# Nine instead of seven pairs of the down projection by block products

## The chip, the cores and the metric

The kernel runs on one core of one Trainium2 chip. Times are device microseconds of one execution. The metric is the median of several executions.

## What is computed

Two transformer blocks over 256 positions of width 2048, all in float32: a first block with two attention layers, and a second one with a mixing layer and a feed-forward layer. The change touches the last product of the feed-forward layer, the down projection:

```python
h = rmsnorm(x, g_ffn[l])                                   # (256, 2048)
u = causal_dwconv(h @ w_up[l], ffn_conv_w[l]) + ffn_conv_b[l]
gate, val = jnp.split(u, 2, axis=-1)
x = x + (jax.nn.silu(gate) * val) @ w_down[l]              # (256, 5632) @ (5632, 2048)
return rmsnorm(x, g_final)
```

## The kernel before

Float32 precision is reached with two rounded parts of each operand. A tile of weights is loaded to a staging buffer, ScalarE rounds it (the part "hi"), VectorE subtracts that from the staged tile (the remainder, "lo"), and TensorE multiplies three passes: activations' hi with weights' hi, hi with lo, lo with hi. A pass is a matmul of a 128x128 block of activations with 128x512 of weights. The activations are in `act_T` with both parts.

The down projection has 44 tiles of 128 rows, taken as 22 row pairs, and 2048 columns, taken as two halves of 1024 (two quarters c of 512 each). PSUM holds 256 positions x 1024 columns at a time: banks `acc[0:2]` for the even quarter of the half, `acc[2:4]` for the odd one.

A pair is done in one of two ways in each half:

- in rows: two units, one for each quarter, each with two tiles x two position blocks x three passes = 12 matmuls. A half needs 24.
- by block products: the pair's 2x2 blocks of activations (two tiles x two position blocks) times its 2x2 blocks of weights (two tiles x two quarters) as seven products instead of eight, three passes each, 21 matmuls. Three products need sums of activation blocks (mixed blocks, `seven_T`, made by VectorE while the up projection of the pair runs, `ffn_sevens`), and four need sums of weight blocks (four VectorE adds of 128x512 in `rest_down`, the pair sums). The four units seven0 to seven3 have 6, 3, 6 and 6 matmuls. Four products go to banks of their own (`aux`), the other three to `acc`.

`DOWN_PAIRS` writes the order out by hand: a list is a group in rows (first all for the even quarter, then all for the odd one), a number is a pair by block products. `down_units` makes the flat list of units j from it. Each engine walks through that list:

- SyncE loads in order: each row unit to one of four staging buffers when the unit four before it has its remainder, each product pair (two transfers of 512 KB) to one of two pair buffers, when the product pair two before has its last remainder. The pair buffers lie where the up projection's activations were, and are free when that is over.
- ScalarE at step j rounds unit j+5 (at the beginning up to two units in a step, `prepared_at`), when its weights are there and TensorE is done with unit j+5-6. At the step after the last product of a half it copies a bank of products. At the step after a quarter's last unit it squares that quarter of x, behind VectorE's add.
- VectorE at step j makes the remainder of unit j+5 (`rest_down`, L692), and for seven1 the four pair sums (L697 to L701). At steps 0 to 2 it ends the last pair of the up projection. At the step after a half's last product it does four adds for the products (`add_sevens`, L2156 to L2159, behind ScalarE's copy), at the next one four more (L2161 to L2164). At a quarter's last unit it adds the two banks to x (`add_to_x`, L458), which frees them.
- TensorE waits for a unit's remainder, and before the first unit of each quarter of the second half also for the banks of the same quarter of the first half (`banks_free`). Before the first product of the second half it waits for `seven_free`, which the last of the eight adds gives.
- GpSimd loads the final gains into `gfin`, 1 MB over all partitions.

A `step(...)` around a VectorE instruction makes the next one wait until it has written.

Of the kernel before, what the change touches and what calls it, by code (L numbers as in the profile page):

```python
# [28 lines left out]
P = 128  # L29
# [93 lines left out]

OUT_PAIRS = [0, 1, 2, 6, 7, 3, 4, 5]

SEVEN = 7
DOWN_PAIRS = 2 * [[[7, 8, 9], 0, [10, 11], 1, [12, 13], 2, [14], 3, [15], 4, [16], 5, [17], 6, [18, 19, 20, 21]]]


def down_units():  # L130
# [70 lines left out]
def build(nc, dram, out):  # L201
# [12 lines left out]
    with ctx:  # L214
        def sb(name, shape, dt=F32, stack=ctx):
            return stack.enter_context(nc.sbuf_tensor("sb_" + name, shape, dt))

        def sem(name):
            return ctx.enter_context(nc.semaphore(name))
# [82 lines left out]
        gate_conv, gate_silu, act_ready = sem("gate_conv"), sem("gate_silu"), sem("act_ready")  # L302
        pair_staged = [sem("pair_staged0"), sem("pair_staged1")]
        sums_ready, first_copied, seven_free = sem("sums_ready"), sem("first_copied"), sem("seven_free")
        last_product = [sem("last_product0"), sem("last_product1")]
        last_added, final_rstd = sem("last_added"), sem("final_rstd")
        final_last = [sem("final_last0"), sem("final_last1")]
# [307 lines left out]
        mixing.close()  # L615


        ffn_tmp = sb("ffn_tmp", [P, 4, 2, SEQ])
        half3, sum3, gate, value = (ffn_tmp[:, i, :, :] for i in range(4))
        gfin = ffn_tmp[:, :, :, :].rearrange("p a c t -> p (a c t)")  # L620
        rb3 = turn_f32[:, 1, 0:T * P].rearrange("p (t k) -> p t k", t=T)
        rbc3 = turn_f32[:, 1, T * P:T * P + SEQ]
        act_T = sb("act_T", [P, FT, 2, SEQ], F32R)
# [79 lines left out]
        with nc.Block() as block:  # L703
# [95 lines left out]
            def _(pool):  # L799
# [77 lines left out]
                    pool.dma_start(pool_w[p0:p0 + n, i, :], w_rows[tile_ * P + p0:tile_ * P + p0 + n, :])\  # L877
                        .then_inc(mix_loaded, 16)

                pool.wait_ge(act_ready, N_FFN)  # L880
                pool.dma_start(gfin[:, :], dram["g_final_2"].partition_broadcast(P)).then_inc(gfin_loaded, 16)


# [1 line left out]
            def _(pe):  # L885
# [358 lines left out]
                def passes(o, a, j, part, start=False, stop=False):  # L1244


                    hi, lo = (ap[:, part * 512:(part + 1) * 512] for ap in down_slot(j))
                    pe.matmul(o, a(0), hi, start=start, stop=False)  # L1248
                    pe.matmul(o, a(0), lo, start=False, stop=False)  # L1249
                    return pe.matmul(o, a(1), hi, start=False, stop=stop)  # L1250
# [11 lines left out]
                def product_seven(j, first, last):  # L1262


                    _, i, _ = DOWN[j]
                    near = lambda k, t: lambda h: act_T[:, 2 * i + k, h, t * P:(t + 1) * P]
                    mixed = lambda n: lambda h: seven_T[:, i, h, n * P:(n + 1) * P]
                    pe.wait_ge(lo_ready, U4 + (j + 1))
                    passes(m_first, near(0, 0), j, 0, first, last)
                    passes(acc[:, 2, :], mixed(2), j, 1).then_inc(unit_used, 1)  # L1270
                    pe.wait_ge(lo_ready, U4 + (j + 2))
                    passes(acc[:, 0, :], near(1, 0), j + 1, 0).then_inc(unit_used, 1)
                    pe.wait_ge(lo_ready, U4 + (j + 3))
                    passes(m_fifth, mixed(0), j + 2, 0, first, last)
                    passes(m_seventh, near(0, 1), j + 2, 1, first, last).then_inc(unit_used, 1)
                    pe.wait_ge(lo_ready, U4 + (j + 4))
                    passes(m_sixth, mixed(1), j + 3, 0, first, last)
                    passes(acc[:, 1, :], near(1, 1), j + 3, 1).then_inc(unit_used, 1)

                for j, (kind, i, c) in enumerate(DOWN[:DOWN_TAIL]):  # L1280
                    if c == 0:
                        pe.wait_ge(act_ready, i + 1)
                    if kind == "rows":
                        first = j == min(r for r in DOWN_ROWS if DOWN[r][2] == c)
                        if first:
                            banks_free(pe, PAIRS4, c)
                        product_down(j, first, j == DOWN_END[c])
                    if kind == "seven0":
                        if j == SEVEN_FIRST[SEVEN]:
                            pe.wait_ge(seven_free, 1)  # L1290
                        product_seven(j, j in (SEVEN_FIRST[0], SEVEN_FIRST[SEVEN]), j + 3 == SEVEN_END[c])
                for t in range(T):
                    o = acc[:, 2 + t, :]
                    for j in range(DOWN_TAIL, U_DOWN):
# [326 lines left out]
            def _(dve):  # L1621
# [527 lines left out]
                def add_sevens(chunk, late):  # L2149
# [10 lines left out]
                    else:  # L2160
# [3 lines left out]
                        dve.tensor_tensor(x_high[1], m_fifth, x_high[1], ALU.add).then_inc(seven_free, 1)  # L2164
                        dve.wait_ge(seven_free, chunk + 1)

                for j in range(U_DOWN):
                    for ahead in prepared_at(j):
                        rest_down(step, dve, ahead)
                    if j == 0:  # L2170
                        ffn_sums(N_FFN, 1, 1)
                    if j == 1:
                        ffn_conv(N_FFN, 1, 1)
                    if j == 2:
                        ffn_act(N_FFN, 1)
                    if j - 1 in SEVEN_END:
                        add_sevens(SEVEN_END.index(j - 1), False)
                    if j - 2 in SEVEN_END:
                        add_sevens(SEVEN_END.index(j - 2), True)
                    if j in DOWN_END[:3]:  # L2180
                        c = DOWN_END.index(j)
                        add_to_x(dve, U4, j, c % 2, c)
# [56 lines left out]
```

## Time and profile before

| | |
|---|---|
| median of 3 runs | 1946.02 us (1945.85 to 1946.25) |
| the profiled execution | 1946.43 us, its span 1944.6 us |
| TensorE busy | 1928.8 us (99%) |
| VectorE busy | 1371.4 us (71%) |
| ScalarE busy | 1047.4 us (54%) |
| down projection | 1704.6 to 1934.6 us of the span |

The span goes from the first to the last instruction. TensorE's matmuls overlap in the records (0.39 us each, a new one every 0.23 us), so their pace is read from start to start.

### The profile page before, as it was taken

The page shows a single profiled execution, that of the slowest core. Times are in us where ns is not written, and L with a number is a line of the kernel's source. Part 1 is how long each engine was busy: PE and PEld are TensorE (multiplying, and loading weights), DVE is VectorE, ACT ScalarE, POOL GpSimd, SP SyncE. Part 2 cuts the span into 40 slices and gives each one's busy share as a digit, 9 for nine tenths or more (in the row PEclk, how much of TensorE's full clock was granted, in tenths as well). Part 3 has the DMA queues.
Part 4 walks back from the last instruction along what each step waited for, and adds up shares of the span by engine and source line. Part 5 has one row for each costly group of instructions (what it writes and reads, how often), then busy time and mean ns, then how long its engine had stood idle before and what let it go on. Part 6 is the DMA issues. An engine that isn't in the chain of part 4 may idle for free.

```text
span 1944.6 us, 27002 instructions
## 1 busy us (share of the span) xinstructions
PE 1928.8 (99%) x9818; PEld 1635.5 (84%) x9818; DVE 1371.4 (71%) x1941; ACT 1047.4 (54%) x1533; POOL 46.4 (2%) x73
## 2 busy tenths in 40 slices
PE   8999999999999999999999999999999999999997
PEld 7888888888888888888888888888888888888886
DVE  7755675656655675656768766888877887888787
ACT  5533676654433676664544544555555555555554
POOL 1000030000000020000100000000000000000000
PEclk9999999999999999999999999999999999999999
DMA  8666545556666555545666545565656566676653
GB/s 310 205 194 194 151 145 160 151 157 186 187 194 192 146 162 174 153 151 180 213 193 188 158 164 186 182 193 184 194 185 193 185 189 188 191 240 203 219 188 117
DMA packets 246964, 357.06 MB, mean 184 GB/s; under 512 B 15318, under 2 KB 136496, under 8 KB 246364
## 3 DMA queue, kind: packets, MB, share of 16 engines
q1 hardware_dynamic: 245148, 349.08, 58.3%
q0 software_dynamic: 1584, 6.54, 1.0%
q8 instruction: 55, 0.90, 0.2%
q14 instruction: 33, 0.27, 0.0%
q10 hardware_dynamic: 144, 0.26, 0.0%
HBM read 352.69 MB, written 3.16 MB: 183 GB/s over the span
## 4 chain that ended last, share of the span: by engine, by line
PE 98%; DMA 1%; DVE 1%; ACT 0%; issue 0%; SPq 0%; ACTq 0%
PE acc L410 22%; PE acc L387 16%; PE acc L389 15%; PE acc L388 15%; PE acc L403 11%; PE acc L1249 3%; PE acc L1250 3%; PE acc L1248 3%; PE aux L467 2%; PE aux L964 1%; DMA sb_stage<-w_kv 1%; PE aux L1249 1%; PE aux L1250 1%; PE aux L1248 1%; PE aux L982 1%; PE aux L945 1%
## 5 line engine op out<-in xcount | busy, mean ns | idle before, releaser
L350 DVE TENSOR_TENSOR sb_w_lo<-sb_stage,sb_w_hi 128x1024 fp32r<-128x1024 f32 x567 | 694.3, 1227 | 377.0 <-ACT sb_w_hi L345 369.9
L345 ACT ACTIVATE sb_w_hi<-sb_stage 128x1024 fp32r<-128x1024 f32 x567 | 598.5, 1058 | 501.5 <-PE acc L389 248.9
L410 PE MATMUL acc<-sb_xT,sb_w_hi 128*128 128x512 f32 x1856 | 445.7, 391 | 0.0
L410 PEld LDWEIGHTS acc<-sb_xT,sb_w_hi 128*128 128x128 f32 x1856 | 340.8, 188 | 65.8
L387 PE MATMUL acc<-sb_w_hi,sb_xT 128*128 128x512 f32 x768 | 305.7, 398 | 0.0
L389 PE MATMUL acc<-sb_w_hi,sb_xT 128*128 128x512 f32 x768 | 299.5, 390 | 0.0
L388 PE MATMUL acc<-sb_w_lo,sb_xT 128*128 128x512 f32 x768 | 299.3, 390 | 0.0
L403 PEld LDWEIGHTS acc<-sb_xT,sb_w_lo 128*128 128x128 f32 x1856 | 238.7, 191 | 9.3
L403 PE MATMUL acc<-sb_xT,sb_w_lo 128*128 128x256 f32 x1856 | 243.0, 283 | 0.0
L387 PE MATMUL acc<-sb_w_hi,sb_mT 128*128 128x512 f32 x560 | 224.7, 401 | 0.8 <-DVE sb_mT L490 0.7
L389 PE MATMUL acc<-sb_w_hi,sb_mT 128*128 128x512 f32 x560 | 218.6, 390 | 0.0
L388 PE MATMUL acc<-sb_w_lo,sb_mT 128*128 128x512 f32 x560 | 218.4, 390 | 0.0
L389 PEld LDWEIGHTS acc<-sb_w_hi,sb_xT 128*128 128x128 f32 x768 | 144.2, 188 | 30.8
L387 PEld LDWEIGHTS acc<-sb_w_hi,sb_xT 128*128 128x128 f32 x768 | 144.3, 188 | 28.7
L388 PEld LDWEIGHTS acc<-sb_w_lo,sb_xT 128*128 128x128 f32 x768 | 144.4, 188 | 27.7
L387 PEld LDWEIGHTS acc<-sb_w_hi,sb_mT 128*128 128x128 f32 x560 | 105.2, 188 | 24.3 <-DVE sb_mT L490 1.3
L389 PEld LDWEIGHTS acc<-sb_w_hi,sb_mT 128*128 128x128 f32 x560 | 105.1, 188 | 22.9
L388 PEld LDWEIGHTS acc<-sb_w_lo,sb_mT 128*128 128x128 f32 x560 | 105.3, 188 | 20.0
L2064 DVE SCALAR_TENSOR_TENSOR sb_ffn_tmp<-sb_ffn_tmp,sb_taps 128x254 f32<-128x254 f32 (+1 forms) x176 | 77.3, 481 | 2.5
L1248 PE MATMUL acc<-sb_w_hi,sb_act_T 128*128 128x512 f32 x192 | 74.7, 389 | 0.0
L1249 PE MATMUL acc<-sb_w_lo,sb_act_T 128*128 128x512 f32 x192 | 74.7, 389 | 0.0
L1250 PE MATMUL acc<-sb_w_hi,sb_act_T 128*128 128x512 f32 x192 | 74.7, 389 | 0.0
(335 smaller groups left out, 1910.5 us busy)
## 6 DMA issues: line engine op xcount, KB each, us to landing
sb_stage<-w_in SPq DMA_DIRECT2D x248, 512.0 KB, 3.9
sb_stage<-w_up SPq DMA_DIRECT2D x176, 512.0 KB, 3.7
sb_stage<-w_out SPq DMA_DIRECT2D x96, 512.0 KB, 4.2
sb_stage<-w_down SPq DMA_DIRECT2D x60, 512.0 KB, 7.0
sb_pair_stage<-w_down SPq DMA_DIRECT2D x28, 512.0 KB, 6.9
sb_stage<-w_kv SPq DMA_DIRECT2D x16, 512.0 KB, 6.8
sb_stage<-w_ukv SPq DMA_DIRECT2D x16, 512.0 KB, 4.0
sb_stage<-w_uq SPq DMA_DIRECT2D x12, 512.0 KB, 3.6
```

The source lines that it names most:

```text
L345: act.activation(w_hi[:, j % RING, 0:size], stage[:, j % RING, 0:size], ACT.Copy).then_inc(hi_ready, 1)
L350: dve.tensor_tensor(w_lo[:, j % RING, 0:size], stage[:, j % RING, 0:size], w_hi[:, j % RING, 0:size].bitcast(F32), ALU.subtract).then_inc( ...
L387: pe.matmul(o, x_hi, hi[:, k, :], start=first and k == 0, stop=False)
L388: pe.matmul(o, x_hi, lo[:, k, :], start=False, stop=False)
L389: mm = pe.matmul(o, x_lo, hi[:, k, :], start=False, stop=last and k == nk - 1)
L403: mm = pe.matmul(acc[:, 2 * pair + c, 0:SEQ], lo[:, k, c * P:(c + 1) * P], xT[:, k0 + k, 0, :], start=False, stop=False)
L410: mm = pe.matmul(acc[:, 2 * pair + c, :], hi[:, k, c * P:(c + 1) * P], both, start=first and k == 0, stop=last and k == 3)
L467: mm = pe.transpose(aux[:, bank, i * P:(i + 1) * P], src(i), ident[:, :])
L1248: pe.matmul(o, a(0), hi, start=start, stop=False)
L1249: pe.matmul(o, a(0), lo, start=False, stop=False)
L1250: return pe.matmul(o, a(1), hi, start=False, stop=stop)
L2064: last = dve.scalar_tensor_tensor(out=y[:, k, d:SEQ], in0=sum3[:, k, 0:SEQ - d], scalar=taps[:, 2 - d, half, k:k + 1], in1=y[:, k, d:SEQ], ...
```

## The change

Nine instead of seven pairs are done by block products in each half. The order is another one: single pairs in rows stand between all products, and the last group of the first half has two pairs instead of four. The mixed blocks of pairs 7 and 8 are not made in the up projection but at steps 4 and 5 of the down stage, by `mix_late`, from the finished activations (hi + lo). They go to a buffer `late_T`, which lies where `ffn_tmp` was. The final gains, which were loaded there, go to the first pair buffer, when the last product pair but one has its last remainder.

```diff
@@ -123,8 +123,9 @@
 
 OUT_PAIRS = [0, 1, 2, 6, 7, 3, 4, 5]
 
-SEVEN = 7
-DOWN_PAIRS = 2 * [[[7, 8, 9], 0, [10, 11], 1, [12, 13], 2, [14], 3, [15], 4, [16], 5, [17], 6, [18, 19, 20, 21]]]
+SEVEN, LATE = 7, 2
+DOWN_PAIRS = [[[9, 10, 11], 0, [12], 1, [13], 2, [14], 3, [15], 4, [16], 5, [17], 6, [18], 7, [19], 8, [20, 21]],
+              [[9], 0, [10], 1, [11], 2, [12], 3, [13], 4, [14], 5, [15], 6, [16], 7, [17], 8, [18, 19, 20, 21]]]
 
 
 def down_units():
@@ -302,6 +303,7 @@
         gate_conv, gate_silu, act_ready = sem("gate_conv"), sem("gate_silu"), sem("act_ready")
         pair_staged = [sem("pair_staged0"), sem("pair_staged1")]
         sums_ready, first_copied, seven_free = sem("sums_ready"), sem("first_copied"), sem("seven_free")
+        late_mixed = sem("late_mixed")
         last_product = [sem("last_product0"), sem("last_product1")]
         last_added, final_rstd = sem("last_added"), sem("final_rstd")
         final_last = [sem("final_last0"), sem("final_last1")]
@@ -615,9 +617,12 @@
         mixing.close()
 
 
+        late = ExitStack()
+        late_T = sb("late_T", [P, LATE, 2, 4 * P], F32R, late)
+        late.close()
         ffn_tmp = sb("ffn_tmp", [P, 4, 2, SEQ])
         half3, sum3, gate, value = (ffn_tmp[:, i, :, :] for i in range(4))
-        gfin = ffn_tmp[:, :, :, :].rearrange("p a c t -> p (a c t)")
+        gfin = pair_stage[:, 0, :, :].rearrange("p a n -> p (a n)")
         rb3 = turn_f32[:, 1, 0:T * P].rearrange("p (t k) -> p t k", t=T)
         rbc3 = turn_f32[:, 1, T * P:T * P + SEQ]
         act_T = sb("act_T", [P, FT, 2, SEQ], F32R)
@@ -877,7 +882,7 @@
                     pool.dma_start(pool_w[p0:p0 + n, i, :], w_rows[tile_ * P + p0:tile_ * P + p0 + n, :])\
                         .then_inc(mix_loaded, 16)
 
-                pool.wait_ge(act_ready, N_FFN)
+                pool.wait_ge(lo_ready, U4 + (SEVEN_FIRST[-2] + 4))
                 pool.dma_start(gfin[:, :], dram["g_final_2"].partition_broadcast(P)).then_inc(gfin_loaded, 16)
 
 
@@ -1264,7 +1269,13 @@
 
                     _, i, _ = DOWN[j]
                     near = lambda k, t: lambda h: act_T[:, 2 * i + k, h, t * P:(t + 1) * P]
-                    mixed = lambda n: lambda h: seven_T[:, i, h, n * P:(n + 1) * P]
+                    if i < SEVEN:
+                        mixed = lambda n: lambda h: seven_T[:, i, h, n * P:(n + 1) * P]
+                        a_third = near(0, 1)
+                    else:
+                        pe.wait_ge(late_mixed, i - SEVEN + 1)
+                        mixed = lambda n: lambda h: late_T[:, i - SEVEN, h, n * P:(n + 1) * P]
+                        a_third = mixed(3)
                     pe.wait_ge(lo_ready, U4 + (j + 1))
                     passes(m_first, near(0, 0), j, 0, first, last)
                     passes(acc[:, 2, :], mixed(2), j, 1).then_inc(unit_used, 1)
@@ -1272,7 +1283,7 @@
                     passes(acc[:, 0, :], near(1, 0), j + 1, 0).then_inc(unit_used, 1)
                     pe.wait_ge(lo_ready, U4 + (j + 3))
                     passes(m_fifth, mixed(0), j + 2, 0, first, last)
-                    passes(m_seventh, near(0, 1), j + 2, 1, first, last).then_inc(unit_used, 1)
+                    passes(m_seventh, a_third, j + 2, 1, first, last).then_inc(unit_used, 1)
                     pe.wait_ge(lo_ready, U4 + (j + 4))
                     passes(m_sixth, mixed(1), j + 3, 0, first, last)
                     passes(acc[:, 1, :], near(1, 1), j + 3, 1).then_inc(unit_used, 1)
@@ -1286,9 +1297,9 @@
                             banks_free(pe, PAIRS4, c)
                         product_down(j, first, j == DOWN_END[c])
                     if kind == "seven0":
-                        if j == SEVEN_FIRST[SEVEN]:
+                        if j == SEVEN_FIRST[SEVEN + LATE]:
                             pe.wait_ge(seven_free, 1)
-                        product_seven(j, j in (SEVEN_FIRST[0], SEVEN_FIRST[SEVEN]), j + 3 == SEVEN_END[c])
+                        product_seven(j, j in (SEVEN_FIRST[0], SEVEN_FIRST[SEVEN + LATE]), j + 3 == SEVEN_END[c])
                 for t in range(T):
                     o = acc[:, 2 + t, :]
                     for j in range(DOWN_TAIL, U_DOWN):
@@ -2164,9 +2175,29 @@
                         dve.tensor_tensor(x_high[1], m_fifth, x_high[1], ALU.add).then_inc(seven_free, 1)
                         dve.wait_ge(seven_free, chunk + 1)
 
+                def mix_late(n):
+
+
+                    i = SEVEN + n
+                    whole, four = turn_f32[:, 0, :], turn_f32[:, 1, :]
+                    step(dve.tensor_tensor(whole.rearrange("p (k t) -> p k t", k=2),
+                                           act_T[:, 2 * i:2 * i + 2, 0, :].bitcast(F32),
+                                           act_T[:, 2 * i:2 * i + 2, 1, :].bitcast(F32), ALU.add))
+                    a11, a21, a12, a22 = (whole[:, k * P:(k + 1) * P] for k in range(4))
+                    first, second, fourth, third = (four[:, k * P:(k + 1) * P] for k in range(4))
+                    step(dve.tensor_tensor(first, a21, a22, ALU.subtract))
+                    dve.tensor_tensor(third, a11, a21, ALU.subtract)
+                    step(dve.tensor_tensor(second, a11, first, ALU.subtract))
+                    step(dve.tensor_tensor(fourth, a12, second, ALU.subtract))
+                    step(dve.tensor_scalar(late_T[:, n, 0, :], four, 1.0, None, ALU.mult))
+                    dve.tensor_tensor(late_T[:, n, 1, :], four, late_T[:, n, 0, :].bitcast(F32), ALU.subtract)\
+                       .then_inc(late_mixed, 1)
+
                 for j in range(U_DOWN):
                     for ahead in prepared_at(j):
                         rest_down(step, dve, ahead)
+                    if j in (4, 5):
+                        mix_late(j - 4)
                     if j == 0:
                         ffn_sums(N_FFN, 1, 1)
                     if j == 1:
```

## Rows read from the trace of the kernel before

**Rows 1.** The page: busy times, the chain that ended last; TensorE's waits.

```profile
PE 1928.8 (99%) x9818; PEld 1635.5 (84%) x9818; DVE 1371.4 (71%) x1941; ACT 1047.4 (54%) x1533; POOL 46.4 (2%) x73
...
PE 98%; DMA 1%; DVE 1%; ACT 0%; issue 0%; SPq 0%; ACTq 0%
...
PE acc L387 <- DVE sb_mT L490: 0.7, 1, 0.7
```

**Rows 2.** Timeline of TensorE, down stage: start, length, instruction, tiles, shapes, count.

```profile
1704.61 0.39 PE L1248 MATMUL acc<-sb_w_hi,sb_act_T 128*128 128x512 f32 x1
...
1725.69 0.39 PE L1248 MATMUL acc<-sb_down_hi,sb_act_T 128*128 128x512 f32 x1
...
1797.77 0.39 PE L1248 MATMUL acc<-sb_w_hi,sb_act_T 128*128 128x512 f32 x1
...
1934.23 0.39 PE L1303 MATMUL acc<-sb_w_hi,sb_act_T 128*128 128x512 f32 x1
```

**Rows 3.** Windows: length, busy PE, PEld, DVE, ACT, POOL (count), clock, DMA, GB/s.

```profile
1715.00:1725.00 10.00, 10.00 (x45) 8.26 (x45) 9.86 (x11) 6.44 (x7) 0.56 (x1) 1.00 0.69 256
...
1765.00:1775.00 10.00, 10.00 (x46) 8.29 (x45) 9.12 (x10) 5.51 (x7) 0.00 (x0) 1.00 0.67 207
```

**Rows 4.** Timeline of VectorE, regular pattern: remainders and pair sums of a product pair.

```profile
1765.13 1.83 DVE L692 TENSOR_TENSOR sb_down_lo<-sb_pair_stage,sb_down_hi 128x1024 fp32r<-128x1024 f32 x2
1766.99 0.69 DVE L697 TENSOR_TENSOR sb_pair_stage<-sb_pair_stage 128x512 f32<-128x512 f32 x1
...
1769.17 0.69 DVE L701 TENSOR_TENSOR sb_pair_stage<-sb_pair_stage 128x512 f32<-128x512 f32 x1
1769.78 2.44 DVE L692 TENSOR_TENSOR sb_w_lo<-sb_pair_stage,sb_w_hi 128x1024 fp32r<-128x1024 f32 x2
```

**Rows 5.** Timeline of VectorE: mixing in the up projection; last activations of the stage.

```profile
1312.89 0.29 DVE L2081 TENSOR_TENSOR sb_turn_f<-sb_ffn_tmp 128x128 f32<-128x128 f32 x1
1313.22 0.29 DVE L2082 TENSOR_TENSOR sb_turn_f<-sb_ffn_tmp,sb_turn_f 128x128 f32<-128x128 f32 x1
...
1713.58 0.43 DVE L2097 TENSOR_SCALAR sb_act_T<-sb_ffn_tmp 128x512 fp32r<-128x512 f32 x1
1714.05 0.69 DVE L2098 TENSOR_TENSOR sb_act_T<-sb_ffn_tmp,sb_act_T 128x512 fp32r<-128x512 f32 x1
1714.65 1.82 DVE L692 TENSOR_TENSOR sb_w_lo<-sb_pair_stage,sb_w_hi 128x1024 fp32r<-128x1024 f32 x2
```

**Rows 6.** Timeline of VectorE, start of the stage: remainders 10 and 11.

```profile
1721.65 2.36 DVE L692 TENSOR_TENSOR sb_down_lo<-sb_stage,sb_down_hi 128x1024 fp32r<-128x1024 f32 x2
```

**Rows 7.** Timelines of VectorE and TensorE: the one wait of TensorE for VectorE.

```profile
9.55 0.69 DVE L490 TENSOR_TENSOR sb_mT<-sb_turn_f,sb_mT 128x512 fp32r<-128x512 f32 x1
...
10.29 0.50 PE L387 MATMUL acc<-sb_w_hi,sb_mT 128*128 128x512 f32 x1 [0.74 <-DVE sb_mT L490]
10.63 0.39 PE L388 MATMUL acc<-sb_w_lo,sb_mT 128*128 128x512 f32 x1
```

**Rows 8.** Timelines, change of halves: ScalarE's rounding (again at the second half's end), VectorE.

```profile
1800.80 1.06 ACT L685 ACTIVATE sb_w_hi<-sb_stage 128x1024 fp32r<-128x1024 f32 x1 [2.38 <-DMA sb_stage<-w_down]
...
1803.04 0.68 DVE L2156 TENSOR_TENSOR sb_turn_f<-aux,sb_turn_f 128x512 f32<-128x512 f32 x1
...
1809.97 1.22 DVE L692 TENSOR_TENSOR sb_w_lo<-sb_stage,sb_w_hi 128x1024 fp32r<-128x1024 f32 x1
...
1812.25 1.28 DVE L458 TENSOR_TENSOR sb_x<-acc,sb_x 128x512 f32<-128x512 f32 x2
1813.44 1.22 DVE L692 TENSOR_TENSOR sb_down_lo<-sb_stage,sb_down_hi 128x1024 fp32r<-128x1024 f32 x1
...
1915.75 1.06 ACT L685 ACTIVATE sb_down_hi<-sb_stage 128x1024 fp32r<-128x1024 f32 x1 [2.35 <-DMA sb_stage<-w_down]
```

**Rows 9.** DMA issues in the down stage: the final gains.

```profile
sb_ffn_tmp<-g_final POOLq DMA_DIRECT2D x1, 1024.0 KB, 7.5
```

**Rows 10.** Window at the end, columns as in rows 3.

```profile
1936.75:1937.00 0.25, 0.00 (x0) 0.00 (x0) 0.22 (x2) 0.00 (x0) 0.00 (x0) 0.50 1.06 426
```

## The prediction

> **What bounds the kernel now.** I read the chain that ended last first: TensorE carries 98% of it, and the summary line of busy times has it busy for 1928.8 of 1944.6 us [rows 1]. A busy TensorE is not yet a TensorE at its pace, so I looked for its waits: in the whole program one is listed against another engine, 0.7 us at the very beginning. The single matmuls of the down projection confirm it [rows 2]. Its first one starts at 1704.61 and the 94th at 1725.69, so one takes 21.08 / 93 = 0.2267 us. The stage has 2 x (7 x 21 + 15 x 24) = 1014 of them (seven block products of three passes for a pair that is done so, 24 matmuls for any other, in each half of the columns); 1014 x 0.2267 = 229.9 us lead from 1704.61 to 1934.5, and the last one does start at 1934.23. There is no gap in this stage, so a matmul taken out is worth its 0.2267 us, as long as what feeds TensorE keeps up. The feeder is VectorE: in ten us of the regular pattern (one pair by products, one in rows) it is busy 9.12 us, and in ten us of the start 9.86 [rows 3]. Where the order gives it less time, it comes last.
>
> I count units as the code does (j from 0 in the down stage). In rows a unit is 12 matmuls, 2.72 us; the four units of a product pair are 6, 3, 6 and 6 matmuls: 1.36, 0.68, 1.36 and 1.36 us, 4.76 together.
>
> **Part 1, fewer matmuls.** Two more pairs of 22 are done with 21 instead of 24, in both halves: 2 x 2 x 3 = 12 matmuls less, 12 x 0.2267 = **-2.72 us**.
>
> **Part 2, the start of the stage.** Units 0 to 9 (six in rows, then pair 0) are the same in both orders. Then the old one has four units in rows, the new one two, and VectorE gets the two mixings between its units 9 and 10 and between 10 and 11. Length of a mixing: an add of 128x512 whose successor waits for it (0.727, the pitch of the pair sums: three of them in 2.18 us) [rows 4], three subtractions of 128x128 with such a wait (0.325 each) and one without (the pitch of an instruction that nobody waits for is its length less 0.09, as 0.69 gives 0.60: 0.29 gives 0.20), a rounding of 0.47 and a rest of 0.60 [rows 5]. Sum 2.97 us, twice 5.94 us. Before, the two unit remainders 10 and 11 follow at once at 1721.65, 1.14 us apart [rows 6]. The new ledger follows. TensorE starts 0.05 us after its operand is there, and the first matmul after a wait takes 0.34 instead of 0.23 us (0.69 us from 9.55 ends at 10.24, starts are 10.29 and 10.63) [rows 7], so every wait costs 0.11 beside its length.
> - Mixing to 1724.62, remainder 10 ready 1725.84; TensorE wants it at 1725.69: +0.20 + 0.11 = 0.31.
> - Mixing to 1728.73, remainder 11 ready 1729.96; wanted at 1725.69 + 0.31 + 2.72 = 1728.72: +1.29 + 0.11 = 1.40.
> - Remainder 12 from 1729.87, remainder 13 and the four pair sums (from its start to the next remainder 1769.78 - 1765.13 - 1.14 = 3.5) [rows 4], remainder 14 ready 1735.75. Wanted at 1732.84 + 1.36 + 0.68 = 1734.88: +0.92 + 0.11 = 1.03.
> - Remainder 15 ready at 1737.0, wanted 1737.27; from here VectorE gains about 1 us in every pattern of 10.2 us.
>
> Together **+2.74 us**. Bounds: 0, if VectorE had the mixings in idle time (it has next to none there [rows 3]), and 3.7 if each of the ten waits inside the mixings costs 0.1 more.
>
> The page "VectorE: DVE Perf Modes" of the Trainium skill, section "The DRAIN you can't avoid", says that a semaphore after every instruction costs nothing against one after the last. The trace disagrees: 0.73 from start to start with the wait, 0.60 without [rows 4, 5]. By the page a mixing would be 2.36 us, the start 1.5 instead of 2.74, and the whole 1.2 us less than I forecast.
>
> **Part 3, the change of halves.** This is the largest term. T is the end of the last product of the first half: 1797.77 in the trace [rows 2]. Four PSUM banks hold the sums of two column quarters, and a quarter of the second half can't begin before VectorE has added the same banks' old sums to x. The old order has 8 units in rows after T, so these banks are wanted at T + 21.8 and T + 29.9. The new one has 4, then the first unit of each new quarter: wanted at T + 10.88 and T + 13.60. VectorE's work from T on is known [rows 8]: the four adds of the products start at T + 5.27 (ScalarE's copy comes behind the rounding of the sixth unit after T, whose weights land at T + 3.0), a remainder behind them at T + 8.2, four more adds end at T + 12.20. In the new order the add of the first quarter follows there, 1.28 long: banks free T + 13.48, TensorE resumes 13.53. Wait 2.65 + 0.11 = **2.76**. The unit that runs then ends at 10.88 + 2.76 + 2.72 = T + 16.36. The other quarter's add waits in VectorE's order behind the 0.69 remainder and the four pair sums of the new half's first pair (from T + 13.39, 3.50) and another remainder (1.14): start T + 18.03, free T + 19.31. Wait 19.36 - 16.36 + 0.11 = **3.11**. Sum **+5.87 us**. What is queued behind, the next products, finds its operands ready (T + 9.4, 14.1, 18.1, 20.4 for units wanted from T + 22.2). Bounds: if those weights landed early, VectorE would begin 2.7 us sooner and the sum be 3.2; if the second add is late by another remainder, 7.1. I take 5.87, since the order of loads up to that point is the same and its nearest row shows the same landing.
>
> **What costs nothing.** The final gains move from a buffer that the mixings now use to a staging buffer; the 1 MB takes 7.5 us [rows 9] and now starts about 30 us before VectorE reads it, with POOL idle. SyncE's pair loads wait for the same event as before; the tightest by the ledger is pair 3's, issued at 1737.0 when remainder 15 frees its buffer and wanted at 1745.7, behind the product of pair 2's first unit: with 7 us to landing it is 1.7 us early, and up to 1 us may come of the row units queued behind it. The new wait for the mixed blocks comes some 65 us after the mixings. End of the stage: the same eight units, the same tail of 10.1 us.
>
> **Sum.** -2.72 + 2.74 + 5.87 = +5.9 us. The profiled execution took 1946.43 us (span 1944.6) and the median of the runs is 1946.02, 0.4 below; from the median 1951.9 us.
>
> **Rivals.**
> - The clock: TensorE stands still for 2.7 and 3.1 us with one unit between them. At the end of the trace the granted clock falls to the lower of its two levels (0.50 of 2.4 GHz) some 2 us after TensorE's last matmul has ended at 1934.6, or sooner [rows 10]. So it may fall here. The unit between the waits is covered by the second; after it one unit at half pace costs 2.7 us more, a half of it as the middle: 1953.3, at most 1954.6. Against: no row shows when it comes back, nor a fall inside the program.
> - The weights of the sixth unit after T land as soon as they are wanted (the wait for a transfer is gone with another traffic): Part 3 is 3.2, total +3.2, 1949.2. Against: the landing at the second half's end, 1915.75, is again 3.1 us behind the last product (411 matmuls after the 507 of the first half end at 1912.7) [rows 8].
> - The other sign: VectorE keeps up everywhere, and only the matmuls count: 1943.3. For it: VectorE is busy 71% of the program, and its lead in the regular pattern is 3.7 us (a remainder ready at 1771.0 [rows 4] for a unit wanted 309 matmuls into the stage, at 1774.7). It decides from the point where the bank adds come before T + 10.9 and the mixings fit in the lead at unit 10, which is 2.8 us before the change. Both fail in the ledgers.
> - The start is as forecast but the change of halves costs nothing, for instance because the adds to x are placed earlier than I read: 1946.0, no change.
>
> "Perfetto Trace Analysis" of the Trainium skill, section "Identifying the Most-Contended Engine", takes occupancy as the measure of a vector engine's room. By that rule the third of these holds, 1943.3 us. The trace's 9.12 of 10 us and the order of single instructions speak against it.
>
> **Chances.** Forecast 0.45, clock 0.25, early weights 0.12, only matmuls 0.08, start alone 0.10. A measurement of this kernel tells about 0.2% (3.9 us) from no change, so slower begins at 1949.9 and faster ends at 1942.1. Slower: forecast, clock and a third of the early weights, 0.74. Faster: half of the matmuls' case, 0.04, should a little more come with them. Same: the rest, 0.22. The range goes from 1949.0 (early weights) to 1954.8 (one unit at half pace).
>
> **What would show it.** TensorE's waits inside the down stage: three short ones at 1725 to 1736 on VectorE's remainders (sum 2.7), two at 1813 to 1830 on VectorE's adds to x (2.7 and 3.0). 1002 matmuls of the stage. The last matmul starting near 1940.1. The granted clock at 1.00 there. Wrong if the waits at the change of halves are missing or over 4 us, or if there is a wait in the regular pattern, which would be a transfer or VectorE's pace.

## The result, and the profile after

The changed kernel takes 1951.0 us (median of 11, 1949.9 to 1952.7), the one before 1946.1 us (median of 11, 1945.5 to 1947.9). The ratio is 1.0028, 95% interval 1.002 to 1.0036: slower by 4.9 us, forecast 5.8, and inside the range. The profiled execution's span is 1949.0 us, 4.4 above the span before.

TensorE's waits for VectorE in the profile after, for the whole program (waiting line, releaser, us in all, times, longest), stand against one of 0.7 us before, at its very beginning [rows 1]. Both programs also wait once for the first load (4.4 and 4.9 us), and the changed one 0.2 us for a transfer ahead of the down projection.

```profile
PE acc L1253 <- DVE sb_x L460: 4.0, 2, 2.6
PE acc L1253 <- DVE sb_down_lo L697: 1.0, 1, 1.0
PE aux L1253 <- DVE sb_w_lo L697: 0.7, 1, 0.7
```

Two on an add to x (L460 is L458 of before), two on a remainder (L697, before L692). The start of the stage on VectorE, answering to [rows 5, 6]; the first mixing goes from 1720.96 to 1723.93:

```profile
1720.96 0.68 DVE L2183 TENSOR_TENSOR sb_turn_f<-sb_act_T 128x512 f32<-128x512 f32 x1
1721.68 0.29 DVE L2188 TENSOR_TENSOR sb_turn_f<-sb_turn_f 128x128 f32<-128x128 f32 x1
1722.01 0.29 DVE L2189 TENSOR_TENSOR sb_turn_f<-sb_turn_f 128x128 f32<-128x128 f32 x1
1722.22 0.28 DVE L2190 TENSOR_TENSOR sb_turn_f<-sb_turn_f 128x128 f32<-128x128 f32 x1
...
1723.32 0.69 DVE L2193 TENSOR_TENSOR sb_late_T<-sb_turn_f,sb_late_T 128x512 fp32r<-128x512 f32 x1
1723.93 1.22 DVE L697 TENSOR_TENSOR sb_down_lo<-sb_stage,sb_down_hi 128x1024 fp32r<-128x1024 f32 x1
```

That is 2.97 us, as forecast, with the pitch of 0.2 where no wait stands (1722.01 to 1722.22) and 0.33 with one. TensorE's timeline beside it, the last matmul before each wait and the first behind it, answering to [rows 2]:

```profile
1724.79 0.39 PE L1255 MATMUL acc<-sb_w_hi,sb_act_T 128*128 128x512 f32 x1
1725.30 0.47 PE L1253 MATMUL acc<-sb_down_hi,sb_act_T 128*128 128x512 f32 x1
...
1727.91 0.39 PE L1255 MATMUL acc<-sb_down_hi,sb_act_T 128*128 128x512 f32 x1
1729.31 0.50 PE L1253 MATMUL acc<-sb_down_hi,sb_act_T 128*128 128x512 f32 x1 [1.01 <-DVE sb_down_lo L697]
...
1734.02 0.39 PE L1255 MATMUL acc<-sb_w_hi,sb_act_T 128*128 128x512 f32 x1
1735.09 0.50 PE L1253 MATMUL aux<-sb_w_hi,sb_seven_T 128*128 128x512 f32 x1 [0.68 <-DVE sb_w_lo L697]
```

The gap is start to start less the pace of 0.23: 0.28, 1.17 and 0.84, with 0.07, 0.11 and 0.11 behind them. A few matmuls behind these are some hundredths late as well, as the sum over the stretch below shows.

Then the change of halves. T, the end of the last product of the first half, is 1809.34 here, where the first matmul in rows starts. ScalarE's rounding of the sixth unit behind it waits for its weights to T + 3.15 (1812.49), and VectorE's adds follow, answering to [rows 8]:

```profile
1812.49 1.06 ACT L690 ACTIVATE sb_w_hi<-sb_stage 128x1024 fp32r<-128x1024 f32 x1 [2.46 <-DMA sb_stage<-w_down]
...
1813.58 1.23 DVE L697 TENSOR_TENSOR sb_w_lo<-sb_stage,sb_w_hi 128x1024 fp32r<-128x1024 f32 x1 [2.30 <-ACT sb_w_hi L690]
1814.72 0.69 DVE L2167 TENSOR_TENSOR sb_turn_f<-aux,sb_turn_f 128x512 f32<-128x512 f32 x1
...
1821.66 1.29 DVE L460 TENSOR_TENSOR sb_x<-acc,sb_x 128x512 f32<-128x512 f32 x2
...
1827.50 1.28 DVE L460 TENSOR_TENSOR sb_x<-acc,sb_x 128x512 f32<-128x512 f32 x2
```

and TensorE:

```profile
1809.34 0.39 PE L1253 MATMUL acc<-sb_down_hi,sb_act_T 128*128 128x512 f32 x1
...
1819.99 0.39 PE L1255 MATMUL acc<-sb_w_hi,sb_act_T 128*128 128x512 f32 x1
1823.00 0.79 PE L1253 MATMUL acc<-sb_w_hi,sb_act_T 128*128 128x512 f32 x1 [2.62 <-DVE sb_x L460]
1823.59 0.63 PE L1254 MATMUL acc<-sb_w_lo,sb_act_T 128*128 128x512 f32 x1
...
1827.06 0.40 PE L1255 MATMUL acc<-sb_w_hi,sb_act_T 128*128 128x512 f32 x1
1828.84 0.50 PE L1253 MATMUL acc<-sb_w_hi,sb_act_T 128*128 128x512 f32 x1 [1.39 <-DVE sb_x L460]
```

The first unit after the first wait is long: its matmuls are 0.43 us apart, and the granted clock says why (windows, columns as in rows 3):

```profile
1822.00:1822.50 0.50, 0.00 (x0) 0.00 (x0) 0.50 (x2) 0.00 (x0) 0.00 (x0) 1.00 0.00 0
1822.50:1823.00 0.50, 0.00 (x0) 0.00 (x1) 0.50 (x2) 0.02 (x1) 0.00 (x0) 0.67 0.00 0
1823.00:1824.00 1.00, 1.00 (x2) 0.83 (x3) 0.97 (x2) 0.97 (x3) 0.00 (x0) 0.50 0.00 0
...
1826.00:1827.00 1.00, 1.00 (x5) 0.79 (x5) 1.00 (x2) 0.65 (x2) 0.00 (x0) 0.96 0.00 0
```

The stage as a whole, with two matmuls behind the waits (the 151st, and the 25th behind the one at 1819.99):

```profile
1703.93 0.39 PE L1253 MATMUL acc<-sb_w_hi,sb_act_T 128*128 128x512 f32 x1
...
1740.66 0.39 PE L1253 MATMUL acc<-sb_down_hi,sb_act_T 128*128 128x512 f32 x1
...
1831.71 0.39 PE L1253 MATMUL aux<-sb_down_hi,sb_act_T 128*128 128x512 f32 x1
...
1939.60 0.39 PE L1314 MATMUL acc<-sb_w_hi,sb_act_T 128*128 128x512 f32 x1
```

At the pace of 0.2267 us, 150 matmuls take 34.00 us and here took 36.73: the start costs 2.73. And 25 take 5.67 and took 11.72: the change of halves costs 6.05. From the first start to the last the stage is 235.67 us against 229.62: +6.05 again, where the steps of the prediction sum to 5.9. The span shows less for two reasons. This execution came 0.7 us sooner to the stage (0.5 of it since its first load landed at 4.4 instead of 4.9 us). And its tail, from the last matmul's start to the end, is 9.4 instead of 10.4 us. This shorter tail is in the profile of every kernel that has the new code for the mixings (9.4 to 9.5 us, in one 10.0), and in neither of the two without it (10.4): a term that the prediction missed, looked at below under the tail. 6.05 - 0.95 = 5.1 us is then what the median should show, and it shows 4.9. The eleven times lie in two groups, six from 1949.9 to 1951.0 and five from 1952.2 to 1952.7, and the median is the highest of the lower group: one more time in the upper one, and it would have been 1952.2. What divides them is looked at under the scatter and the clock.

### The profile page after: what moved, and what is told of

Read it like the earlier page. It is cut to its first block, busy times and chain, and to the rows that moved or that the text cites. A ratio compares the mean times of both kernels' runs of the same rounds, so it can differ in the third digit from the quotient of the medians.

```text
span 1949.0 us, 27032 instructions
## 1 busy us (share of the span) xinstructions
PE 1929.6 (99%) x9806; PEld 1635.3 (84%) x9806; DVE 1394.7 (72%) x1979; ACT 1051.8 (54%) x1541; POOL 46.3 (2%) x73
## 4 chain that ended last, share of the span: by engine, by line
PE 96%; DVE 3%; DMA 0%; ACT 0%; issue 0%; SPq 0%; ACTq 0%
PE acc L412 22%; PE acc L389 16%; PE acc L391 16%; PE acc L390 16%; PE acc L405 11%; PE aux L469 2%; PE acc L1253 2%; PE acc L1254 2%; PE acc L1255 2%; PE aux L1253 1%; PE aux L1254 1%; PE aux L1255 1%; PE aux L969 1%; PE aux L950 1%; PE aux L987 1%; PE aux L986 1%
## 5 line engine op out<-in xcount | busy, mean ns | idle before, releaser
L690 ACT ACTIVATE sb_w_hi<-sb_pair_stage 128x1024 fp32r<-128x1024 f32 (+1 forms) x54 | 52.4, 986 | 67.5 <-DVE sb_pair_stage L703 57.3
L697 DVE TENSOR_TENSOR sb_w_lo<-sb_pair_stage,sb_w_hi 128x1024 fp32r<-128x1024 f32 (+1 forms) x54 | 60.3, 1132 | 0.4
L1571 ACT ACTIVATE sb_ffn_tmp<-sb_ffn_tmp,sb_taps 128x256 f32<-128x256 f32 x88 | 48.1, 595 | 17.9 <-DVE sb_ffn_tmp L2067 17.1
```

The costliest lines, as they stand in the source:

```text
L697: dve.tensor_tensor(lo, src, hi.bitcast(F32), ALU.subtract).then_inc(lo_ready, 1)
```

## The experiments

In the tables and below, "stage" is the time from the start of the down projection's first matmul to that of its last, read in TensorE's timeline of each profile. It leaves out the scatter ahead of the stage and behind it. The kernels were timed in turn with the kernel before, 6 to 11 times each; the two single runs only once.

| kernel | stage, us | stage against before | median, us | before beside it |
|---|---|---|---|---|
| before | 229.62 |  | 1946.1 |  |
| changed | 235.67 | +6.05 | 1951.0 | 1946.1 |
| changed again | 235.60 | +5.98 | 1951.1 | 1946.1 |
| changed, two single runs | 236.72, 236.73 | +7.10, +7.11 | 1952.3, 1951.7 | 1946.1 |
| mixings at 30 and 42 | 236.24 | +6.62 | 1951.7 | 1946.1 |
| short group alone | 234.99 | +5.37 | 1952.8 | 1946.1 |
| mixings alone | 231.40 | +1.78 | 1947.1 | 1946.1 |
| mixings at 12 and 30 | 232.64 | +3.02 | 1949.3 | 1946.0 |
| adds first | 231.53 | +1.91 | 1947.0 | 1946.0 |
| both | 228.77 | -0.85 | 1944.3 | 1946.0 |
| room | 227.90 | -1.72 | 1943.8 | 1946.0 |
| copy first | 234.73 | +5.11 | 1950.4 | 1946.1 |
| room, copy first | 226.89 | -2.73 | 1942.6 | 1946.1 |

**The start alone.** The old order and number of products, with the two mixings at steps 4 and 5:

```diff
-DOWN_PAIRS = [[[9, 10, 11], 0, [12], 1, ...
+DOWN_PAIRS = 2 * [[[7, 8, 9], 0, [10, 11], 1, [12, 13], 2, [14], 3, ..., 6, [18, 19, 20, 21]]]
```

> The kernel before in order and number of products, with the two mixings of the change at steps 4 and 5, their results not used, and the final gains in the pair buffer. Theory: the first two waits of the start ledger, 0.31 and 1.40 us; the third is gone, since units 12 and 13 are in rows: 1.7 us more than before, 1947.8 us. Rival 1: the four units in rows give VectorE room and the mixings cost nothing, 1946.1. Rival 2: moving the final gains costs at the end of the stage, then a wait near 1929 us, and more than 2 us.

Stage +1.78 us, with two waits of 0.28 and 1.29 us and their 0.08 each: the ledger's first two, and not its third. The median is 1.1 us above before (ratio 1.0005, 0.9996 to 1.0014), which its interval does not tell from nothing, so it is the stage that carries this verdict; 1.8 less 0.95 of the tail would be 0.8. Moving the final gains left no wait at the end: rival 2 is out.

**The change of halves alone.** The kernel before with its rows in another order:

```diff
-DOWN_PAIRS = 2 * [[[7, 8, 9], 0, [10, 11], 1, [12, 13], 2, [14], 3, [15], 4, [16], 5, [17], 6, [18, 19, 20, 21]]]
+DOWN_PAIRS = [[[7, 8, 9], 0, [10, 11], 1, [12, 13], 2, [14, 15], 3, [16, 17], 4, [18], 5, [19], 6, [20, 21]],
+              [[7], 0, [8, 9], 1, [10, 11], 2, [12, 13], 3, [14, 15], 4, [16], 5, [17], 6, [18, 19, 20, 21]]]
```

> The kernel before (seven pairs by products, no mixing in the stage) with the order of its rows changed alone: two instead of four pairs stand behind the last product of the first half, one instead of three at the beginning of the second. The same matmuls, the same VectorE work. Theory (the banks are wanted before VectorE has added them to x): two waits of TensorE for the adds to x, 2.76 and 3.11 us, 5.9 us more than before, about 1952.0 us (1953.6 where the clock stays low). Rival (VectorE's load of two more product pairs in each half is what costs): the load is that of before, the time 1946.1.

1952.8 us, ratio 1.0033 (1.0021 to 1.0045), with the same 1014 matmuls and the same VectorE work. The stage is 5.4 us longer, and TensorE's timeline has just two waits, both for the adds to x (L459 here):

```profile
1821.18 0.59 PE L1249 MATMUL acc<-sb_down_hi,sb_act_T 128*128 128x512 f32 x1 [1.93 <-DVE sb_x L459]
...
1827.02 0.50 PE L1249 MATMUL acc<-sb_down_hi,sb_act_T 128*128 128x512 f32 x1 [1.24 <-DVE sb_x L459]
```

So the place of the four units in rows costs this, not the two further products. The profile is of the shortest of the six executions (1951.39), and its stage with the tail of before accounts for it; the median is 1.4 us above it, and no trace shows one of the longer ones.

**Mixings later.** In the changed kernel:

```diff
-                    if j in (4, 5):
+                    if j in (30, 42):
```

> The changed kernel with the two mixings at steps 30 and 42 instead of 4 and 5. Theory: VectorE has about 3.7 us of lead there, a mixing takes 2.95, so the three waits at the start go and nothing new comes: 2.7 us less than the changed kernel, about 1948.3 us, five waits become two. Rival (the order itself, with single pairs in rows from the start, is too dense for VectorE): the start waits stay and the time is that of the changed kernel, 1951; second rival: the lead is used up at the new place, a wait of 1 to 2 us appears there, and the gain is 1 us.

A miss. The three waits at the start did go, and a wait of 0.25 us came at pair 7. But the time stayed, 1951.7: the wait for the first bank had grown.

```profile
1818.18 0.39 PE L1255 MATMUL acc<-sb_w_hi,sb_act_T 128*128 128x512 f32 x1
1824.00 0.80 PE L1253 MATMUL acc<-sb_w_hi,sb_act_T 128*128 128x512 f32 x1 [5.43 <-DVE sb_x L460]
```

ScalarE's timeline of the same profile shows the way there; T is 1807.5, and the last three roundings before the copy (L1613) all wait for weights:

```profile
1807.65 1.06 ACT L690 ACTIVATE sb_w_hi<-sb_stage 128x1024 fp32r<-128x1024 f32 x1 [0.22 <-DMA sb_stage<-w_down]
1810.46 1.06 ACT L690 ACTIVATE sb_w_hi<-sb_stage 128x1024 fp32r<-128x1024 f32 x1 [1.74 <-DMA sb_stage<-w_down]
1813.49 1.06 ACT L690 ACTIVATE sb_w_hi<-sb_stage 128x1024 fp32r<-128x1024 f32 x1 [1.97 <-DMA sb_stage<-w_down]
1814.45 0.58 ACT L1613 ACTIVATE sb_turn_f<-aux 128x512 f32<-128x512 f32 x1
```

The mixing at step 42 had put VectorE's remainders back. These free the staging buffers: the one that frees the sixth unit's buffer ended at T - 0.1 instead of T - 2.2, the load went out 2.1 us later, and it landed at T + 6.0 instead of T + 3.1. I took the second mixing away from there:

```diff
-                    if j in (4, 5):
+                    if j in (12, 30):
```

> The changed kernel with the mixings at steps 12 and 30. With the second one at step 42 the three waits at the start went, but the wait for the first bank grew from 2.8 to 5.6 us. Theory A: the mixing at 42 took VectorE's lead two patterns ahead of the change of halves, a pair load stood behind it in SyncE's order with the row loads behind that, and the sixth unit's weights landed at T + 6.0 instead of T + 3.0. With the second mixing at 30 the lead is there again: waits at the start 0 (some tenths at most), at the change of halves 2.8 and 3.1 (the second shorter by the slow unit), the stage 232.9 us, 2.7 less than in the changed kernel, time 1948.4 (1950 where the clock stays low). Rival B: at the change of halves VectorE has a fixed amount of work to do by a fixed time, and the waits at the start only moved it; then the first bank's wait grows again by what the start saves, and the time is 1951.

Stage 232.64, 3.0 us less than the changed kernel; the only waits left are the two for the banks, 2.5 and 1.4 us with a slow unit between. Median 1949.3. The sixth unit's weights landed at T + 2.8. Theory A holds, rival B falls: the start's waits are worth their length, if the second mixing stands where the lead can be won back. With four product pairs still to come in the half (step 30) it was, with two (step 42) it was not; no place between was tried.

**The order at the change of halves.** In VectorE's program (the same calls leave their old places further down, not shown; ScalarE's squares of the two quarters go behind, with a wait for `seven_free`):

```diff
+                    if j == SEVEN_END[0] + 2:
+                        add_to_x(dve, U4, DOWN_END[0], 0, 0)
+                    if j == SEVEN_END[0] + 3:
+                        add_to_x(dve, U4, DOWN_END[1], 1, 1)
+                        dve.wait_ge(acc_free[1], PAIRS4 + 1)
+                        add_sevens(0, True)
                     for ahead in prepared_at(j):
                         rest_down(step, dve, ahead)
```

> The changed kernel with VectorE's order at the change of halves turned: the adds of the first quarter to x directly behind the first four adds of the products, those of the second quarter before the last four, ScalarE's squares of both later. VectorE's work is the same. Theory: bank 0 is free at T + 9.4 (wanted 10.9) and bank 1 at T + 12.4 (wanted 13.6), so both waits go; the last four adds end at T + 15.2, the pair sums follow, and the new half's first product waits for its third unit: wanted T + 18.4, ready 19.9, 1.7 us with its 0.11. The start waits stay. In all 4.2 us less than the changed kernel, about 1946.9 us, no clock fall. Rival: the banks are not it but the work VectorE has to do between the halves; then 5.9 us of waits stay in another place, 1951.

1947.0 us, stage 231.53 (expected 231.5). Both waits for the banks are gone, and in their place stands the one that was expected, for the third unit of the first product:

```profile
1829.82 0.50 PE L1253 MATMUL aux<-sb_w_hi,sb_seven_T 128*128 128x512 f32 x1 [1.57 <-DVE sb_w_lo L697]
```

The banks were it. Both edits together:

> Both edits, mixings at 12 and 30 and the adds to x first. Theory: the terms add up: -2.72 for the matmuls and the 1.7 left at the change of halves, 1.0 us less than before: about 1945.1 us. Rival: what one edit saves the other loses; 1947 or more.

1944.3 us, stage 228.77, 0.85 less than before; 0.95 of the tail comes to it, and the median is 1.7 less (ratio 0.9992, 0.9983 to 1.0001, which alone does not tell it from no change). Then the room in front of the second half's first product (pair 6's load goes out one row unit earlier, and the last four adds of the products stand between the two adds to x again):

```diff
-              [[9], 0, [10], 1, [11], 2, [12], 3, [13], 4, [14], 5, [15], 6, [16], 7, ...
+              [[9, 10], 0, [11], 1, [12], 2, [13], 3, [14], 4, [15], 5, 6, [16], 7, ...
```

> As both edits, and in the second half pairs 9 and 10 in rows stand before the first product, while the products of pairs 5 and 6 follow each other without rows between (pair 6's load is then issued one row unit earlier). The last four adds of the products come before the second quarter's add again. Theory: bank 0 free T + 9.4 (wanted 10.9), bank 1 free T + 15.7 (wanted 16.3), the product's third unit ready T + 21.4 (wanted 23.8): no wait at the change of halves, and the double product takes 2.1 us of VectorE's lead of 3.7. Only the 12 matmuls are left: 2.7 us less than before, 1943.4 us. Rival: the double product or its loads make a wait of 1 to 3 us, 1945 to 1946.

1943.8 us, ratio 0.9989 (0.998 to 0.9998). The double product makes no wait. But the ledger missed 1.0 us of the stage: TensorE still waits 0.56 + 0.11 for the second bank, since VectorE starts its adds at T + 6.3 here and not at T + 5.3, and 0.16 + 0.11 at 1925, at the end of the second half. VectorE is late there too: its last add of bank sums to x starts 1.6 us behind the last matmul's start, and 1.0 in the kernel with the copy first as well, and by this 0.55 us the tail of this kernel is longer.

**The late weights.** ScalarE's copy and VectorE's first four adds go ahead of the sixth unit:

```diff
+                    if j - 1 in SEVEN_END:
+                        multiplied(act, U4, j - 1)
+                        act.activation(first_f, m_first, ACT.Copy).then_inc(first_copied, 1)
                     for ahead in prepared_at(j):
                         round_down(act, ahead)
```

> The changed kernel, with ScalarE's copy of a product bank at the end of a half put ahead of the rounding that waits for the weights landing at T + 3.0, and VectorE's first four adds ahead of that unit's remainder. Theory (the 2.8 us for late weights are a term of both waits at the change of halves): the adds start at T + 0.9 instead of T + 5.3, bank 0 is free at T + 10.5 (wanted 10.9, no wait), bank 1 at T + 16.4 (wanted 13.6): one wait of 2.9 us instead of 2.8 and 3.1. Start waits as before. 3.0 us less than the changed kernel: about 1948.3 us, stage 232.7 us. Rival (VectorE's amount of work sets it, its start does not): no change, 1951.2.

A hit in the waits and a miss in the time. The waits are 0.51 + 0.11 and 2.98 us: the weights are a term of the first one, as forecast, but 0.6 is left, for VectorE stood one unit earlier than I had it (the fifth unit's remainder comes first and waits for its own weights; the adds start at T + 2.0, not 0.9). The stage is 234.73, not 232.7, since there is this 0.6, and since the matmuls behind the second wait run at the lower clock in this profile (1.3 us). The 11 times lie in two groups, 1948.5 to 1948.6 (three) and 1950.2 to 1951.4 (eight): the lower one is where the expectation was, but no trace shows one of the three. With the room it leaves nothing:

> The kernel with both edits and room before the first product (1943.8 us, one wait of 0.7 us left for the second bank), and the copy first as well. Theory: bank 1 is free 3 us sooner, that wait goes, the stage is 1002 matmuls without a gap, 227.1 us, and the time 1943.1 us. Rival: the copy first delays the sixth unit's rounding and a wait comes there; 1943.8 or more.

1942.6 us (1942.2 to 1942.8), ratio 0.9982 (0.9973 to 0.9991), 3.5 us faster than before. Of TensorE's waits in the whole program only the one for the first load is left, and 1001 x 0.2267 is 226.9:

```profile
PE acc L894 <- DMA sb_qb<-par_rows: 4.8, 1, 4.8
```

**The tail.** In the profiled executions the span ends 10.4 us behind the start of the last matmul in the kernel before and in the one with the short group alone, and 9.4 to 9.5 us in all others but "room" (10.0). The difference between 10.4 and 9.4 arises behind ScalarE's last instruction, which ends 5.7 us behind the last matmul's start in either; so the final gains' new place is not its cause. The DMA view of the last 8 us (queues with packets, MB, share; then issues with the us to landing), first of the kernel with the short group alone, whose program is that of before in all else:

```profile
q14 instruction: 1, 0.01, 0.8%
...
out<-sb_x SPq DMA_DIRECT2D x3, 256.0 KB, 2.7
out<-sb_x ACTq DMA_DIRECT2D x1, 256.0 KB, 3.2
```

then of the changed one, where the queue of instruction loads has no packet in this stretch:

```profile
out<-sb_x SPq DMA_DIRECT2D x3, 256.0 KB, 2.3
out<-sb_x ACTq DMA_DIRECT2D x1, 256.0 KB, 2.8
```

With a load of instructions among the last stores (its packet starts 6.7 us behind the last matmul's start and takes 1.0 us), the first store lands as before, the next two 0.4 us later, the last one 1.0 us later, and so does the end; the kernel before has the same packet and the same 3.2. In the kernel with the mixings alone the packet comes 1.5 us ahead of the last matmul's start, and the tail is 9.4. That the packet is the cause, and that the longer program moved it away, is argued from this coincidence over the profiles; no kernel was made to test it alone.

**The scatter and the clock.**

> The changed kernel once more, for the spread of its times (they lie in two groups, near 1950.8 and near 1952.4 us). Theory (VectorE is late at two places): five waits of TensorE in the down stage as predicted, 2.7 us in all at the start and 5.9 us at the change of halves, in every execution. The clock falls during the first wait for the banks and comes back before the second one ends, which costs nothing in the profiled execution; in the executions of the upper group it comes back late or falls again in the second wait, and some 8 matmuls behind it start 0.43 instead of 0.23 us apart, +1.6 us. Rival: the spread comes from the landings of the weights; then the waits themselves differ between the groups.

> The changed kernel, one look for the spread of its times (1950 to 1952.7 us, while kernels without the waits for banks spread half as wide). If the time is over 1952: theory, the waits are the same and matmuls behind the second wait run at the lower clock; rival, a wait is longer. If it is under 1951.5: the clock is back before the second wait ends.

> A second look at the changed kernel, with the same expectations: over 1952 us with matmuls at the lower clock behind the second wait (theory) or with a longer wait (rival); under 1951.5 us with neither.

The first profile was taken at 1951.15 us and shows what the first one of the change showed. The single runs, at 1952.25 and 1951.68, show the other kind. From TensorE's timeline (T is 1809.63), ScalarE's rounding of the sixth unit and the windows of the first of them:

```profile
1809.63 0.39 PE L1253 MATMUL acc<-sb_down_hi,sb_act_T 128*128 128x512 f32 x1
...
1822.72 0.50 PE L1253 MATMUL acc<-sb_w_hi,sb_act_T 128*128 128x512 f32 x1 [2.04 <-DVE sb_x L460]
...
1828.55 0.69 PE L1253 MATMUL acc<-sb_w_hi,sb_act_T 128*128 128x512 f32 x1 [2.78 <-DVE sb_x L460]
1829.04 0.63 PE L1254 MATMUL acc<-sb_w_lo,sb_act_T 128*128 128x512 f32 x1
...
1831.60 0.63 PE L1254 MATMUL acc<-sb_w_lo,sb_act_T 128*128 128x512 f32 x1
```

```profile
1812.20 1.06 ACT L690 ACTIVATE sb_w_hi<-sb_stage 128x1024 fp32r<-128x1024 f32 x1 [1.90 <-DMA sb_stage<-w_down]
```

```profile
1823.00:1824.00 1.00, 1.00 (x5) 0.76 (x5) 0.95 (x2) 0.97 (x4) 0.00 (x0) 1.00 0.00 0
...
1828.00:1829.00 1.00, 0.45 (x1) 0.40 (x2) 1.00 (x2) 0.47 (x1) 0.00 (x0) 0.85 0.00 0
1829.00:1830.00 1.00, 1.00 (x4) 0.77 (x3) 0.63 (x1) 0.97 (x4) 0.00 (x0) 0.50 0.00 0
```

After the first wait the clock is still up, the unit behind it has its normal length, the second wait is 2.9 us, and now the clock falls as it ends: seven matmuls and the one before run at half pace in the open. The stage is 236.7, 1.1 us longer than where the slow unit hides in the second wait. Theory and rival were each half right. The landings do differ between the kinds: the sixth unit's weights were there at T + 2.6 in both single runs and at T + 3.1 in the two profiles of the other kind, and with them both banks were free 0.6 us sooner (TensorE resumes at T + 13.1 and T + 18.9 instead of 13.7 and 19.5). By this the single runs should be shorter. They are longer, since the slow matmuls now stand where nothing covers them: from the second resumption on the stage loses 1.75 us instead of 0.15. So the clock costs 1.6 us, the sooner landing gives 0.6 back, and 1.0 to 1.1 is left. Why the clock fell in the first wait here and in the second there, no run shows. One remark in the expectation does not hold as it stands: kernels without such waits do not all scatter half as wide, for the kernel before spreads over 2.4 us in the eleven runs beside the changed one. The last kernel's eleven lie within 0.7.

## Why the prediction was right

- What bounds it: held. TensorE had no slack to give, and every wait went into the stage one for one, but for what another covered.
- Part 1, 12 matmuls, -2.72: held. The stage has 1002 matmuls, and in the last kernel it is just 2.73 us shorter than before.
- Part 2, +2.74: 2.73 by the pace, 2.58 of it in the three waits and the matmul behind each, each within 0.13 us of its forecast; the length of a mixing was exact. With the mixings moved, the stage was 3.0 shorter, 0.3 of it at the change of halves. The ledger's 0.12 us for each wait inside VectorE is in it; by the rule of the Trainium skill ("VectorE: DVE Perf Modes", section "The DRAIN you can't avoid") a mixing would have been 2.36 us, and the trace with its 2.97 does not agree.
- Part 3, +5.87: 6.05. The order of events was the forecast one, all of it 0.1 to 0.2 us late after T: weights at T + 3.1 (3.0), adds from T + 5.4 (5.3), second bank free at T + 19.4 (19.3). The size was right, but its path was not in full: the first wait was 2.78 (2.76), the unit behind it 1.6 us slower, and the second wait with the matmul behind it 1.66 in place of 3.11. The slow unit was covered by the wait that it shortened, as the clock rival has it.
- The clock rival: not an alternative but an addition. "The granted clock at 1.00 there" was wrong: it fell in all four profiles of the changed kernel. By the profiles this costs nothing where the second wait covers it, and 1.6 us in the other kind, where I had given 1.35 as the middle. That the median is the last of the lower group and not the first of the upper is luck.
- "The same tail of 10.1 us": wrong. From the last matmul's start to the end it is 0.95 us shorter than before. The stage came out 0.15 us over its sum, so this and the place of the median in its lower group are why the median is 0.9 us under the forecast; the cause of the shorter tail is argued only.
- The early weights, no wait at the change of halves, and only the matmuls: all three are out by the landing at T + 3.1 and the five waits. The rule of occupancy in the Trainium skill ("Perfetto Trace Analysis", section "Identifying the Most-Contended Engine") would have given 1943.3: VectorE was busy 72% and yet late at two places. With the order repaired and the same VectorE work, 1942.6 was reached. So the room was there on the average, and the order decided whether it was where it was needed.

## What to carry to other kernels

A saving on the bounding engine is worth its pace only as long as each feeder keeps its lead; take the ledger of the feeder at the two places where its work is not regular, the start of a stage and the change of accumulator banks. Where banks are reused, put the reads that free them ahead of everything on that engine that nobody is waiting for yet. Work put into a feeder's lead is only free where enough regular patterns follow to win the lead back, because its lead also decides when the loads go out.

## What the runs showed of the hardware

- The granted clock fell to 0.50, the lower level, at standstills of TensorE of 1.9 (short group alone), 2.3 (mixings at 12 and 30), 2.5 to 2.8 and 5.4 us in the midst of a dense stage: 2.3 us after the last matmul's end in the changed kernel (1820.4 to 1822.7), 2.9 in the first single run. It stayed up through standstills of 2.0 and 2.1 in the two single runs, so their length alone did not decide it; none of 1.0 to 1.6 us showed it. Behind it 5 to 7 matmuls in a row followed at 0.43 instead of 0.23 us (10 behind the longest), which cost 1.6 us of the stage where nothing covered it.
- A load of instructions among the last stores goes with an end 1.0 us later (tail 10.4 against 9.4 us); a coincidence over fourteen profiles, not tested alone.
- A wait inside VectorE cost 0.12 us between instructions of 128x512 and of 128x128 alike (start to start 0.73 against 0.60, 0.33 against 0.21).
